# Value rows of the expert layer: nearly all added by DVE, those beside routing by PE, and ACT makes the coefficients and diagonals

## What is computed

```python
x = x + attention_branches(x)
xb = rmsnorm(x)
q = (xb @ wq).reshape(n, 8, 2, 128)
sc = einsum("nhpc,hpkc->nhpk", q, subkeys)
s1, i1 = top_k(sc[:, :, 0], 16)
s2, i2 = top_k(sc[:, :, 1], 16)
top_s, pos = top_k(s1[..., :, None] + s2[..., None, :], 16)
g = softmax(top_s)
act = gelu(einsum("nhkd,nd->nhk", u[eidx], xb))
x = x + einsum("nhk,nhkd->nd", g * act, v[eidx])
```

## Time and profile before

| what | us |
|---|---|
| median of 3 runs | 2659.16 |
| lowest, highest | 2646.86, 2667.52 |
| span of the profiled execution, its own time | 2671.0 |

### The profile page before, as it was taken

The page is one execution under the profiler, slowest core; times in us unless marked ns, Lnnn a source line. Parts: engine busy times, 40 slices in busy tenths (PEclk is TensorE's granted clock), DMA queues, the critical chain, the costliest instruction groups (busy, mean ns, idle before and its releaser), DMA issues. The chain is left out here.

```text
span 2671.0 us, 23686 instructions
## 1 busy us (share of the span) xinstructions
PE 2152.5 (81%) x7804; PEld 1230.3 (46%) x7804; DVE 1434.8 (54%) x3480; ACT 524.8 (20%) x1354; POOL 671.1 (25%) x694
## 2 busy tenths in 40 slices
PE   7989889987698876897887778888765898987766
PEld 6845566455346632444562234456322344664211
DVE  0111105654554397666448865654795566337956
ACT  2321111110341101441110133301111332010111
POOL 0000000233222133233223422322333223223433
PEclk9988999999678987888998887999987787778788
DMA  9832455798769987678999866799989567888887
GB/s 275 272 91 86 136 185 173 290 361 316 266 231 333 331 322 298 257 272 325 367 376 334 346 243 247 299 378 334 396 308 387 221 248 285 304 310 310 313 329 314
DMA packets 271239, 765.82 MB, mean 287 GB/s; under 512 B 22736, under 2 KB 191744, under 8 KB 201488
## 3 DMA queue, kind: packets, MB, share of 16 engines
q0 software_dynamic: 78336, 570.46, 55.6%
q1 hardware_dynamic: 156848, 155.52, 18.6%
q10 hardware_dynamic: 35936, 38.35, 4.3%
HBM read 745.56 MB, written 18.30 MB: 286 GB/s over the span
## 5 line engine op out<-in xcount | busy, mean ns | idle before, releaser
L1217 PE MATMUL acc<-ring,diag 128*128 128x512 f32 (+1 forms) x1720 | 950.3, 705 | 272.2 <-DVE diag L1563 264.7
L600 POOL DMA_INDIRECT ring<-in_uv,stage x544 | 614.0, 1129 | 1471.1 <-PE acc L1217 877.0
L1552 DVE CUSTOM_DVE_ANT_0 ring<-ring,xb 128x1024 f32<-128x1024 f32 x544 | 651.5, 1221 | 209.1 <-DMA ring<-in_uv,stage 199.7
L1217 PEld LDWEIGHTS acc<-ring,diag 128*128 128x128 f32 (+1 forms) x1720 | 362.2, 222 | 783.4 <-issue 425.9
L898 ACT ACTIVATE gel<-dots 128x1 f32<-128x1 f32 x544 | 105.6, 201 | 1059.0 <-DVE dots L1552 1040.8
L1563 DVE TENSOR_SCALAR diag<-ident,gel,gw 128x128 f32<-128x128 f32 x406 | 141.8, 357 | 213.0 <-ACT gel L898 200.7
L1001 PE MATMUL pz<-F,wbuf 128*128 128x416 f32 (+1 forms) x656 | 244.8, 533 | 3.6 <-issue 1.4
L1001 PEld LDWEIGHTS pz<-F,wbuf 128*128 128x128 f32 (+1 forms) x656 | 127.1, 196 | 114.7 <-issue 114.7
L618 POOL COPY stage<-idx 128x4 int32<-128x4 int32 x130 | 50.9, 392 | 505.6 <-DVE gw L1511 486.6
L1411 DVE TENSOR_REDUCE nmax<-ps 128x1 f32<-128x128 f32 (+4 forms) x72 | 35.6, 495 | 236.9 <-PE ps L1058 81.5
L1577 DVE SCALAR_TENSOR_TENSOR vsum<-ring,coefd,vsum 128x1024 f32<-128x1024 f32 x109 | 140.3, 1287 | 4.0
(11 more groups left out here) (259 smaller groups left out, 1954.4 us busy)
## 6 DMA issues: line engine op xcount, KB each, us to landing
wbuf<-in_w_in SPq DMA_DIRECT2D x52, 1024.0 KB
wbuf<-in_peer_wq SPq DMA_DIRECT2D x40, 1024.0 KB
wbuf<-in_w_pa SPq DMA_DIRECT2D x20, 1024.0 KB
wbuf<-in_w_o SPq DMA_DIRECT2D x20, 1024.0 KB
wbuf<-in_w_pb SPq DMA_DIRECT2D x20, 512.0 KB
ring<-in_uv,stage POOLq DMA_INDIRECT x544
zT<-F ACTq DMA_DIRECT2D x28, 208.0 KB, 2.9
qT<-zT ACTq DMA_DIRECT2D x4, 768.0 KB, 6.8
```

Source lines behind the costliest of these rows:

```text
L600: pool.indirect_dma_start(out=ring[:, slot, :], out_offset=None, in_=d["uv"], in_offset=bass.IndirectOffsetOnAxis(ap=stage[:, a, k:k + 1], ...
L1217: last = nc.tensor.matmul(acc[0:nq, c * 512:(c + 1) * 512], diag[:, parity, 0:nq], ring[:, slot, D + c * 512:D + (c + 1) * 512], start=Fal ...
L1552: nc.vector.tensor_tensor_reduce(out=u, in0=u, in1=xb[:, t % 2, :], scale=1.0, scalar=0.0, op0=ALU.mult, op1=ALU.add, accum_out=dots[:, sl ...
```

## The change

The table of adders has a new rule. In tiles 0 to 3 PE adds slots 76 to 119 (blocks 19 to 29) as before, and DVE all others, 84 in a tile. In the last tile they take turns. DVE has 352 slots, PE 192.

The coefficient is made by ACT for every slot, right behind the gelu (`weigh`, a copy with a scale of one number per partition, into `cf`), and for PE's slots ACT also makes the diagonal (a copy of the identity with the coefficient as scale). DVE keeps the dots and its adds. ACT waits for its own results between these steps, and DVE's add waits for the coefficient. The loop of the last tile is gone; its slots stand in the plan like the others.

```diff
@@ adder_counts
     for s in range(SLOTS * (TILES - 1) + SLOTS // 4):
-        who_early = "vector" if s < BLOCK * EARLY and s % BLOCK else None
-        late = s < SLOTS * (TILES - 1) and LATE[0] <= s % SLOTS // BLOCK < LATE[1]
-        who = "vector" if s % BLOCK == BLOCK - 1 and not late else "tensor"
-        who = who_early or who
+        if s < SLOTS * (TILES - 1):
+            who = "tensor" if ROUTING[0] <= s % SLOTS // BLOCK < ROUTING[1] else "vector"
+        else:
+            who = "tensor" if s % 2 else "vector"
@@ scalar engine
+            def weigh(t, s, j):
+                slot = s % RING
+                act.wait_ge(gelued, s + 1)
+                nc.scalar.activation(cf[:, slot:slot + 1], gel[:, slot:slot + 1], ACT.Copy, scale=gw[:, t % 2, j:j + 1]
+                                     ).then_inc(weighed, 1)
+                who, n = ADDERS[s]
+                if who == "tensor":
+                    nq = rows_of(t)
+                    pick = ident if t < TILES - 1 else sel32
+                    if n > DIAGS:
+                        act.wait_ge(v_added, n - DIAGS)
+                    act.wait_ge(weighed, s + 1)
+                    nc.scalar.activation(diag[:, (n - 1) % DIAGS, 0:nq], pick[:, 0:nq], ACT.Copy,
+                                         scale=cf[:, slot:slot + 1]).then_inc(coef_set, 1)
...
+                for j in range(j0, j0 + HALF):
+                    gelu(SLOTS * t + j)
+                    weigh(t, SLOTS * t + j, j)
@@ vector engine
-            def weigh(t, slot, parity, g, gelus, adds):
...
-                nc.vector.tensor_scalar(diag[:, parity, 0:nq], pick[:, 0:nq], gel[:, slot:slot + 1], g,
-                                        ALU.mult, ALU.mult).then_inc(coef_set, 1)
...
-                dve.wait_ge(gelued, gelus)
-                c = coefd[:, turn:turn + 1]
-                nc.vector.tensor_scalar(c, gel[:, slot:slot + 1], g, None, ALU.mult).then_inc(coefd_set, 1)
+                slot, n = s % RING, ADDERS[s][1]
+                dve.wait_ge(weighed, s + 1)
+                v, c = ring[:, slot, D:2 * D], cf[:, slot:slot + 1]
...
+                half = range(SLOTS * t + j0, SLOTS * t + j0 + HALF)
+                for s in half:
+                    dot(t, s)
+                for s in half:
+                    if ADDERS[s][0] == "vector":
+                        add_v(t, s)
```

More of the change, by code:

```diff
@@ L58 @@
 DIAGS = 9
-EARLY = 11
-LATE = (19, 30)
+ROUTING = (19, 30)
 STAGES = 3
@@ L195, in make_plan @@
             plan += [("pack", t + 1, 0), ("finish", t, 0)]
-    return plan + [("experts_loop", TILES - 1, 0), ("finish", TILES - 1, 0)]
+    plan += [("experts", TILES - 1, b) for b in range(SLOTS // 4 // HALF)]
+    return plan + [("finish", TILES - 1, 0)]
 def cols_of_group(g):
@@ L627, in experts @@
                     gather(k, a, s % RING, waits)
[L629 to L651, removed]
             for what, t, b in PLAN:
@@ L894, in pack_sample, with gelu @@
                     act.dma_start(xb[pp, t % 2, :], xb[0:DEC, t % 2, :]).then_inc(packed, 16)
-            def gelu(slot, count):
-                act.wait_ge(dotted, count)
+            def gelu(s):
+                slot = s % RING
+                act.wait_ge(dotted, s + 1)
                 nc.scalar.activation(gel[:, slot:slot + 1], dots[:, slot:slot + 1], ACT.Gelu).then_inc(gelued, 1)
-            def experts(t, b, h):
[L901 to L912, removed]
-                experts(t, blocks - 1, 0)
-                experts(t, blocks - 1, 1)
+            def weigh(t, s, j):
+                slot = s % RING
+                act.wait_ge(gelued, s + 1)
[10 more added lines that the diff above has]
+                                         scale=cf[:, slot:slot + 1]).then_inc(coef_set, 1)
+            def experts(t, b, h):
+                j0 = BLOCK * b + HALF * h
+                if j0 == 0:
+                    act.wait_ge(route_ready, t + 1)
+                    if t == TILES - 1:
+                        act.wait_ge(packed, 16 * 9)
+                for j in range(j0, j0 + HALF):
+                    gelu(SLOTS * t + j)
+                    weigh(t, SLOTS * t + j, j)
             def finish(t):
@@ L1259, in _ @@
             for what, t, p in PLAN:
-                if what in ("experts", "experts_loop") and held:
+                if what == "experts" and held:
                     experts(*held)
@@ L1546, in front, with dot @@
                     top(t, p - TOP)
-            def dot(t, slot, landed):
-                dve.wait_ge(row_landed[slot], landed)
+            def dot(t, s):
+                slot = s % RING
+                dve.wait_ge(row_landed[slot], 16 * (s // RING + 1))
                 u = ring[:, slot, 0:D]
@@ L1566, in add_v @@
[L1566 to L1573 removed]
+            def add_v(t, s):
+                slot, n = s % RING, ADDERS[s][1]
+                dve.wait_ge(weighed, s + 1)
+                v, c = ring[:, slot, D:2 * D], cf[:, slot:slot + 1]
+                if n == v_adds("vector", SLOTS * t) + 1:
@@ L1574, in add_v @@
                     last = nc.vector.tensor_scalar(vsum[:, :], v, c, None, ALU.mult)
                 else:
[L1576 removed]
+                    dve.wait_ge(v_added_dve, n - 1)
                     last = nc.vector.scalar_tensor_tensor(vsum[:, :], v, c, vsum[:, :], ALU.mult, ALU.add)
                 last.then_inc(v_added_dve, 1)
[L1580 to L1602 removed]
@@ L1604, in experts @@
             def experts(t, b, h):
-                if b == 0 and h == 0:
+                j0 = BLOCK * b + HALF * h
+                if j0 == 0:
                     dve.wait_ge(route_ready, t + 1)
```

66 lines of the change are left out of this document (3 added, 63 removed).

## The result

The changed kernel takes 2831.82 us as a median of 4 runs (2819.48 to 2834.91), against 2661.97 us for the kernel before on the same chip (4 runs). The ratio is 1.066, with a 95% interval of 1.062 to 1.070: 6.6% slower. The forecast was 2697 us with a range of 2615 to 2765. The direction was right; the size was not, and the time lies above the range. The span of the profiled execution is 2832.6 us, 161.6 more than before.

A forecast was written before the change was run, and what follows sets the result against it. Taken as bounds: DVE's chain in attention, nearly full DVE in routing, DMA in projections and last tile. 104 + 12 + 33 − 45 − 44 − 14 − 8 = +38 on 2671.0: 2709, as median 2697 us (2615 to 2765).

The forecast's parts named there:

- Adds in attention: Beside attention, slots moved from PE to DVE lengthen DVE's chain, with nothing to cover them: +104 us (0 to 104).
- The waits in attention (33 − 45): DVE's waits for attention scores: +33 us from PE's slower clock, −45 us given back in FoX steps.
- PE's clock: In attention, PE without its adds runs more bias steps at the slow clock: +33 us (0 to 60).
- The 55%: Part taken of the 60 us that all attention bias steps at the slow clock would cost, giving +33.
- PE goes cold: Rival: in attention all bias steps are slow and FoX scores keep most of their wait; 2749 us as median, chance 0.20.
- FoX steps: In attention, PE without adds does a step's first scores during DVE's dots, shortening waits: −45 us (−20 to −72).
- ACT's coefficient: In attention's score steps, DVE waits some 0.25 us for ACT's coefficient behind the gelu: +12 us (0 to 24).
- Routing: Beside routing, diagonals leave DVE's chain, with the gain limited by DMA's free share: −44 us (−20 to −68).
- Projections, first slots, last tile: Projections −14 us as PE is relieved in tile 3; first 44 slots −8; last tile 0, at the DMA wall.
- Rival 1: PE's queued adds hold up ACT and DVE, so every return is at its far end: 2603 us as median, chance 0.20.
- Rival 3: Gathers set the pace, so attention's added time returns in routing and projections: no change, near 2659 us, chance 0.20.

The follow-up runs named there:

- act_alone: Changed kernel with the old rule of adders, so only ACT's coefficients and diagonals are new; 2624.73 us, ratio 0.985 to the kernel before.
- table_alone: Kernel before with only the new table of adders (old pattern in tile 3's last block and the last tile); 2858.53 us, ratio 1.074.
- zero_half: Changed kernel plus one PE matmul of zeros for each slot that DVE adds beside attention; 2819.02 us, ratio 1.061.
- zero_adds: Changed kernel plus two PE matmuls of zeros for each slot that DVE adds beside attention; 2771.36 us, ratio 1.039.
- after_defer: Changed kernel with DVE's two adds in each attention score step moved behind the merge, ahead of the maxima; 2702.28 us, ratio 1.016.
- attention_all_pe: Changed kernel with the old rule of adders, except that PE adds every slot beside attention; 2554.83 us, ratio 0.961.

## Why the prediction was right in direction and wrong in size

The 885.7 us of attention can be put beside the other kernels as DVE busy plus DVE idle (us, each from the sum of the four stretches):

| kernel | attention | DVE busy | DVE idle | clock of tile 1 |
|---|---|---|---|---|
| before | 690.7 | 408.8 | 281.9 | 0.83 |
| act_alone | 686.8 | 364.4 | 322.4 | 0.86 |
| changed | 885.7 | 514.9 | 370.8 | 0.51 |
| table_alone | 882.4 | 541.0 | 341.4 | 0.50 |
| zero_half | 863.9 | 515.2 | 348.7 | 0.67 |
| zero_adds | 814.8 | 515.4 | 299.4 | 0.80 |
| after_defer | 756.2 | 510.2 | 246.0 | 0.53 |
| attention_all_pe | 625.3 | 314.4 | 310.9 | 0.95 |

**Adds in attention (+104): right.** DVE's busy time rose by 106.1 us, in tile 1 by 28.7 where 28.4 was forecast. That nothing covers it was right too, and after_defer shows why: the order on DVE, not its load, puts the adds on the path.

**The waits in attention (33 − 45): the step that failed.** The forecast let what PE's slower clock costs and what the FoX steps give back nearly cancel. DVE's idle time before the maxima of the scores, summed over the four attentions from its timeline, grew by 89.6 us:

| DVE idle before | before | changed | difference | forecast |
|---|---|---|---|---|
| first bias score of an attention | 37.2 | 51.3 | +14.1 | |
| other bias scores | 108.1 | 162.8 | +54.7 | +33 |
| first score of a FoX step | 31.5 | 18.7 | −12.8 | −45, with the row below |
| second score of a FoX step | 53.8 | 87.4 | +33.6 | |

**PE's clock (+33): mis-sized.** The price of a slow bias step was right: 15 us per tile or 60 in all had been worked out for the case that every step is slow, and 54.7 were measured. The 55% failed. It came from a mix of the two levels before; in the changed kernel tile 1 stood at 0.51 over the whole attention, and no pair of waits was a fast one. The reading of PE's load was off too. 705 ns is the mean length of one matmul, but these overlap: PE's adds kept it busy for 69 us of tile 1's attention and not for 93 (the table by stretch before, with the instructions of L1217 alone, so the first two busy times are PE and PEld):

```profile
1055.50:1223.20 167.70, 68.95 (x132) 27.93 (x132) 0.83 0.73 275
```

So 74 us stayed with it and not 50, and at the lower clock they became the 112.12 that were measured where 90 or less were forecast. The zeros took back 71 us of attention, and I put at least that much down to the clock, since the zeros cost PE time as well. The Trainium skill (TensorE: Matmul & The Clock Gate, Part 1) says that the slow clock is PE's default and that activity releases it. The trace agrees, with 0.50 to 0.53 in all four attentions. The forecast had named this as the rival "PE goes cold", whose 2749 us came nearest but was still 83 short: it had the bias steps right and gave the FoX steps −20, where +21 was measured.

**FoX steps (−45): wrong in sign, the largest miss.** The forecast said that the scores come late because two slots' adds stand ahead of them on PE. That holds for the first score of a step only: without adds PE runs ahead to it, and its wait fell by 12.8 us. The second score has another chain, and its wait is the larger part. PE first multiplies the values of the step before, and for that it waits for DVE's store (L1371), which stands behind DVE's adds; then come transposes and scores. In the changed kernel, PE and then DVE:

```profile
1240.08 1.51 PE L1073 MATMUL po<-vb,F 128*128 128x64 f32 x6 [7.01 <-DVE F L1371]
...
1242.16 1.65 PE L1018 MATMUL pz<-kbT,qT 64*128 64x384 f32 x2
1243.73 1.64 PE L1037 MATMUL pz<-ckey,x 16*128 16x384 f32 x2
...
1246.14 0.56 DVE L1376 TENSOR_REDUCE nmax<-pz 128x1 f32<-128x384 f32 x1 [5.75 <-PE pz L1040]
```

The same place before, at a clock of 1.00:

```profile
1200.91 0.78 PE L1091 MATMUL po<-vb,F 128*128 128x64 f32 x6
...
1201.95 0.91 PE L1036 MATMUL pz<-kbT,qT 64*128 64x384 f32 x2
...
1204.15 0.56 DVE L1411 TENSOR_REDUCE nmax<-pz 128x1 f32<-128x384 f32 x1 [2.49 <-PE pz L1058]
```

The same work takes 1.65 us instead of 0.91, and the wait is 5.75 instead of 2.49. So the clock's price is in the FoX steps too, where the forecast gave it no share. attention_all_pe bears out both halves: with more adds on PE the first waits grew to 59.6 us over the four attentions, and at the full clock the second waits in tile 1 are 2.49 again.

**ACT's coefficient (+12): about right in this kernel.** DVE's adds beside attention waited 31.5 us for coefficients (11.3 of it in one wait beside tile 3), where before 15.8 were waited for gelus. In act_alone it is 9.7 us in tile 1 and 53.8 in all four, and that took back nearly all of the 44.4 us by which DVE's work fell there.

**Routing (−44): it came to −2.8.** The diagonals did leave DVE: 111.73 to 100.01 us busy in tile 1, 11.7 less, and 42 in all four routings. But DVE's idle time there grew by 39, so DVE's load wasn't the bound that the forecast took it for. The stretch is 5.6 shorter in tile 1 and 8.8 longer in tile 3. DVE's waits in the routing of tile 1 and of tile 3:

```profile
DVE ring L1518 <- DMA ring<-in_uv,stage: 13.9, 9, 3.5
DVE F L1403 <- ACT F L850: 8.8, 1, 8.8
```

```profile
DVE F L1403 <- ACT F L850: 27.2, 1, 27.2
```

The wait at L1403 is for the key scores that ACT stores at the end of the projections; before, DVE had 4.5 and 19.6 us of waits for gelus in these stretches. Over the four routings the key scores cost 59 us of waits, where before there was none, and gathered rows 47 instead of 28, while 40 us of waits for gelus went. In act_alone, with the diagonals on ACT too, the four routings came to 495.9, −6. So the term was too large even without the table. Why tile 3's key scores come so late was not tested.

**Projections, first slots, last tile (−14, −8, 0): right in sum**, at −16.5, −11.4 and −2.9. For the projections a part of that is luck: beside tile 3, which the −14 was worked out for, it was −12.6, and −9.7 beside tile 0, +1.4 and +4.5 beside tiles 1 and 2 were not forecast. DVE waited 26.8 us for late coefficients in tile 1's projections.

In sum: the adds were right with 106 us; waits in attention came to 89 where the sum had 0 (12 + 33 − 45), 66 of it in the FoX term alone; and the routing was 41 short. Rival 1 (PE in the way) falls by the changed kernel, yet attention_all_pe shows the opposite of its reason: more on PE is faster. Rival 3 (gathers set the pace) falls as well. DMA's share in tile 1's attention fell to 0.56. (The range's lower end of 2615 is rival 1's span; as a median that rival came to 2603, outside the range.)

One thing stays open. In the first step of attention in tile 1 PE waited 9.7 us for the queries `qT`: the load took 12.7 us from issue to landing and 6.6 before, by the view of that tile. It is a part of the +14.1 us of the first bias scores. Tiles 2 and 3 had longer loads too, and so had zero_adds at its higher clock (a first wait of 10.4). The DMA engines had a mean share of 1.02 while this load was under way and of 0.78 before. In tile 1 it took 9.7 to 15.6 us at shares of 0.89 to 1.02 in the five kernels that add every slot beside attention on DVE, and 5.3 to 6.6 at 0.79 to 0.87 in the seven others. So it seems to share the DMA engines with gathers that now fall beside it; no run moved the one without the other.

## What to carry to other kernels

Before moving work from a nearly full engine to a half idle one, ask which of the two stands in the chain that the other engines wait on. Here DVE, busy 54%, was the chain beside attention, and PE, busy 81%, mostly stood idle when DVE handed it a merge. Where an engine has waits and also independent work, put that work inside the waits: the order alone was worth 130 us here. And count what the remaining work of the relieved engine will run at: PE's share of attention at 1.2 GHz cost some 70 us, which no sum of the instruction times of before shows. Last, follow each wait by itself: the two scores of a FoX step looked alike and had different chains.

## What the runs showed of the hardware

Useless work on PE made the kernel faster: 2771 us with two zero matmuls per slot, 2819 with one, 2832 with none, at mean granted clocks of 0.80, 0.67 and 0.51 in tile 1's attention. A mean between 0.50 and 1.00 is a mix of stretches at the two levels, and what counts is the level while the scores are made: at one zero matmul per slot the second waits of all eight bias steps were still the slow 2.17 us.

The issue of a gather by GpSimd took 1129 ns on average before (109 adds of this form on DVE), 1132 in attention_all_pe (68) and 1280 in the changed kernel (347). In the changed kernel 181 gathers with neither a dot nor an add beside them took 1.01 us on average, the other 363 1.41 us. The Trainium skill (SBUF — State Buffer, SBUF: two separate sides) states that a DVE operation with two SBUF inputs and a GpSimd operation that reads SBUF lock each other out for a whole instruction. The trace agrees in direction, but 0.4 us is less than a whole instruction of 1.28. Why it is so little no run here shows, nor whether this lock is the reason. It should have cost little here, since POOL had been waiting for DVE's adds before most gathers (1013.6 us in the row of L598).
